# Norm sums of 256 columns in two matmuls, norms begun by chunks' first terms, and attention's last branch in two halves

## The reference

```python
def rms_norm(x, w):                       # rmsnorm of the second block is the same
    return x * lax.rsqrt(jnp.mean(x * x, axis=-1, keepdims=True) + 1e-6) * w

def hybrid_mixer(h, w_in, dn_conv, ...):  # layers 0 and 1
    proj = h @ w_in
    (dn_qkv, dn_z, dn_b, dn_a, ret_q, ret_k, ret_v, ret_g, pool_u, gates) = split(proj)
    qkv = silu(causal_depthwise_conv(dn_qkv, dn_conv))      # 1536 features
    beta = sigmoid(dn_b)
    g = -exp(dn_A_log) * softplus(dn_a + dn_dt_bias)
    ...                                   # delta rule, retention, pooling: o_dn, o_ret, o_pool
    y = gt[0] * (o_dn @ w_branch_dn) + gt[1] * (o_pool @ w_branch_pool) + gt[2] * (o_ret @ w_branch_ret)
    return y @ w_out

def first_block(x, ...):
    for l in range(2):
        m = hybrid_mixer(rms_norm(x, mix_pre_norm[l]), ...)
        x = x + rms_norm(m, mix_post_norm[l])
        h = rms_norm(x, ffn_pre_norm[l])
        x = x + rms_norm((silu(h @ w_gate) * (h @ w_up)) @ w_down, ffn_post_norm[l])
    return x

def hybrid_mixer_2(u, pos, w_in, ..., w_a, w_b, w_c, w_o):   # layers 2 and 3
    ...                                   # three attentions: o_a, o_b, o_c
    g = sigmoid(gates)                    # 3 x 1024 features
    merged = g[0] * (o_a @ w_a) + g[1] * (o_b @ w_b) + g[2] * (o_c @ w_c)
    return merged @ w_o

def second_block(h, ...):
    for l in range(2):
        h = h + hybrid_mixer_2(rmsnorm(h, attn_norm[l]), ...)
        u = rmsnorm(h, mlp_norm[l])
        h = h + square(relu(u @ w_up[l])) @ w_down[l]
    return rmsnorm(h, final_norm)
```

## Time and profile before

| what | value |
|---|---|
| time, median of 3 runs | 1926.45 us (1924.01 to 1933.04) |
| the profiled execution: its time | 1926.13 us |
| its span in the trace | 1924.3 us |
| PE busy | 1887.5 us, 98% |
| ACT, DVE, POOL busy | 50%, 64%, 15% |
| waits of PE for other engines, all | about 30 us |

### The profile page before, as it was taken

How to read it: one execution, slowest core, us unless ns; L and a number is a source line. 1 busy time by engine, 2 the same in 40 slices (tenths; PEclk the granted TensorE clock), 3 DMA queues, 4 the chain that set the end, 5 groups by cost and what they waited for, 6 DMA issues and landing times.

```text
span 1924.3 us, 35105 instructions
## 1 busy us (share of the span) xinstructions
PE 1887.5 (98%) x14820; PEld 1800.8 (94%) x14820; DVE 1237.3 (64%) x1669; ACT 961.8 (50%) x1383; POOL 295.6 (15%) x168
## 2 busy tenths in 40 slices
PE   7999999999999999999999999999999999999998
PEld 7999998998899999999988999999999999999998
DVE  6874566665589545767647675577646684567643
ACT  5533455444563345554445445655534444656633
POOL 0050221000003103200001352310000353220000
PEclk9999999999999999999999999999999999999999
DMA  6443344656455323655665553446655663345663
GB/s 232 158 145 104 120 152 136 214 194 208 134 162 165 110 99 121 208 174 180 194 199 177 176 183 121 132 154 202 192 186 172 215 194 120 131 158 182 194 196 104
DMA packets 92156, 317.50 MB, mean 165 GB/s; under 512 B 11744, under 2 KB 12896, under 8 KB 91744
## 3 DMA queue, kind: packets, MB, share of 16 engines
q1 hardware_dynamic: 91424, 314.69, 50.1%
q10 hardware_dynamic: 576, 0.57, 0.1%
HBM read 304.99 MB, written 1.05 MB: 159 GB/s over the span
## 4 chain that ended last, share of the span: by engine, by line
PE 84%; DVE 11%; ACT 3%; issue 1%; DMA 0%; SPq 0%; DVEq 0%; ACTq 0%
PE bank L1901 82%; DVE wlo L1076 5%; DVE area L1076 3%; ACT area L618 1%; DVE area L1082 1%; ACT whi L624 1%; PE bank L2367 1%; PE bank L2099 1%; DMA raw<-in_weights 0%; DVE area L1562 0%; DVE area L1079 0%; DVE area L1560 0%; PE bank L2385 0%; ACT hh L618 0%; DVE hl L1082 0%
## 5 line engine op out<-in xcount | busy, mean ns | idle before, releaser
L1076 DVE TENSOR_TENSOR wlo<-raw,whi 128x1024 fp32r<-128x1024 f32 x518 | 659.0, 1286 | 422.1 <-ACT whi L624 421.5
L1901 PE MATMUL bank<-hh,whi 128*128 128x256 f32 x2928 | 834.6, 285 | 20.6 <-DVE wlo L1076 12.9
L1901 PE MATMUL bank<-hl,whi 128*128 128x256 f32 x2928 | 817.6, 279 | 0.0
L1901 PE MATMUL bank<-hh,wlo 128*128 128x256 f32 x2928 | 817.5, 279 | 0.0
L624 ACT CAST whi<-raw 128x1024 fp32r<-128x1024 f32 x572 | 589.0, 1046 | 403.2 <-PE bank L1901 378.0
L1901 PEld LDWEIGHTS bank<-hh,whi 128*128 128x128 f32 x2928 | 556.2, 190 | 36.2 <-DVE wlo L1076 16.8
L1901 PEld LDWEIGHTS bank<-hl,whi 128*128 128x128 f32 x2928 | 554.9, 190 | 2.0 <-issue 1.9
L1901 PEld LDWEIGHTS bank<-hh,wlo 128*128 128x128 f32 x2928 | 554.7, 189 | 0.0
L1691 POOL TENSOR_TENSOR area<-area 128x512 f32<-128x512 f32 (+4 forms) x90 | 136.9, 1530 | 1010.2 <-ACT area L618 678.8
L1901 PE MATMUL bank<-area 128*128 128x128 f32 (+5 forms) x1544 | 200.2, 289 | 1.0 <-DVE area L1130 0.7
L1691 POOL TENSOR_TENSOR wlo<-raw,whi 128x1024 fp32r<-128x1024 f32 x54 | 134.2, 2487 | 429.8 <-ACT whi L624 429.8
(11 more groups left out here) (124 smaller groups left out, 1887.4 us busy)
## 6 DMA issues: line engine op xcount, KB each, us to landing
raw<-in_weights SPq DMA_DIRECT2D x572, 512.0 KB, 4.0
area<-area SPq DMA_DIRECT2D x96, 64.0 KB, 3.8
area<-area SPq DMA_DIRECT2D x16, 128.0 KB, 3.9
cst<-in_const SPq DMA_DIRECT2D x1, 1188.0 KB, 6.1
cst<-in_const SPq DMA_DIRECT2D x1, 1024.5 KB, 5.7
xT<-in_x SPq DMA_DIRECT2D x4, 256.0 KB, 8.0
out<-xT SPq DMA_DIRECT2D x4, 256.0 KB, 2.9
area<-in_lev SPq DMA_DIRECT2D x2, 384.0 KB, 5.7
```

The source lines that it names most:

```text
L1076: return v.tensor_tensor(dst, x, y, op)
L1901: return e.matmul(ps, x, y, start=start, stop=stop, skip_group_check=skip)
```

## The change

It has four parts.

1. *Norm sums.* The squares are added down to 256 columns before PE sees them (three additions of 1024, 512 and 256 columns on DVE for the norms in `SUMMED`, else four on POOL), and `norm_sum` is two matmuls of 128 columns. It stands after the fourth chunk instead of the second; the first two evacuations wait for it. In qkv the SW matmuls and the start of the delta rule stand two chunks later as well.
2. *Transitions* (norms in `TURNED`). PE takes the first two chunks together, part by part, first only the terms with hh (`parts`), then the terms with hl. DVE makes all eight additions and then lows 1 to 3; POOL makes low 0. ACT splits one chunk before the highs and one between highs and squares (`AROUND`).
3. *Last branch.* B2H and B2L are made in two halves, from turns 8 and 9 apart, in buffers of their own; PE's first wc chunk takes the first half for both its tiles, then the second (`last_branch`). wb's last evacuations come before the splits of their step.
4. *Gates.* sigmoid(x) is (tanh(x/2) + 1)/2: ACT makes tanh, DVE multiplies the bank by gate + 1, and the factor 1/2 goes into FH and FL. Tanh and Exp are taken from one table set in attention.

```diff
 # ACT
+                if fn is AF.Tanh:
+                    tables(EXPTANH)
+                elif fn is AF.Ln or fn is AF.Exp and table[0] != EXPTANH:
                     ln_exp()
...
-                    if hook and len(chunks) == 2:
+                    if hook and step < 2:
+                        waiting, done = waiting + done, []
+                    if hook and step == 2:
                         hook()
+                        done = waiting + done
...
+                split(around[0])
                 for j in range(4):
                     high(then, j, *v_norm.at("added", then, j))
+                split(around[1])
                 for j in range(4):
+                    if j == 3:
+                        a.wait_ge(*g_norm.at("low", then))
                     square(then, j)
...
+            def gate(name, L, j):
+                projection, dst = BRANCH[name][2:]
+                a.wait_ge(*v_evac.at(projection, L, 2 * j + 2))
+                d = dst[:, 512 * j:512 * j + 1024]
+                act(d, d, AF.Tanh, scale=0.5).then_inc(*a_br.up("gate", name, L, j))
...
+                def wc_high(j):
+                    a.wait_ge(*a_att.at("OO", L, 8 + j))
+                    a.copy(BR2[0][:, 2 * j:2 * j + 2, :], v3(BRANCH["wc"][1])[:, 2 * j:2 * j + 2, :]).then_inc(*a_br.up("high", "wc", L, j))
 # DVE
+            def squares(norm):
+                v.wait_ge(*a_norm.at("square", norm, 3))
+                for n in (4 * T, 2 * T, T):
+                    x = tt(SQ2[:, 0:n], SQ2[:, 0:n], SQ2[:, n:2 * n], OP.add)
...
+                for j in range(4):
+                    add(j)
+                for j in range(1, 4):
+                    low(then, j)
...
-                    tt(gate[:, c], b[:, :], gate[:, c], OP.mult).then_inc(*v_evac.up(name, L, m0))
+                    stt(gate[:, c], gate[:, c], 1.0, b[:, :], OP.add, OP.mult).then_inc(*v_evac.up(name, L, m0))
 # POOL
+            def low(norm):
+                g.wait_ge(*a_norm.at("high", norm, 0))
+                for k in (0, 1):
+                    x = g.tensor_scalar(SQ2[:, (6 + k) * T:(7 + k) * T], xT[:, k, :], GAIN[norm][:, k:k + 1], None, OP.mult)
+                x.then_inc(*g_norm.up())
+                g.wait_ge(*g_norm.now())
+                tt(hl[:, 0:2, :], v3(pair(SQ2, 3)), hh[:, 0:2, :].bitcast(F32), OP.subtract).then_inc(*g_norm.up("low", norm))
 # PE
+            def parts(job, ready, norm):
...
+                for k in range(8):
+                    e.wait_ge(*(a_norm.at("high", norm, k // 2) if k else a_norm.at("first", norm)))
+                    for m in range(2):
+                        i = (at + m) % RING
+                        mm(bank[b][:, m * T:(m + 1) * T], whi[:, i, 128 * k:128 * k + 128], hh[:, k, :], (m, k) == (0, 0), False, True)
+                        mm(bank[b][:, m * T:(m + 1) * T], wlo[:, i, 128 * k:128 * k + 128], hh[:, k, :], False, False, True)
+                for j in range(4):
+                    e.wait_ge(*ready(j))
+                    for m in range(2):
+                        for k in (2 * j, 2 * j + 1):
+                            x = mm(bank[b][:, m * T:(m + 1) * T], whi[:, (at + m) % RING, 128 * k:128 * k + 128], hl[:, k, :], False, k == 7, True)
...
-                for j in (1, 3):
-                    e.wait_ge(*g_norm.at("squares", norm, j))
-                    for k in range(2):
-                        x = mm(bank[b][:, 0:T], C("ones"), pair(SQ2, j)[:, k * T:(k + 1) * T], (j, k) == (1, 0), (j, k) == (3, 1))
+                e.wait_ge(*(v_norm if norm in SUMMED else g_norm).at("squares", norm))
+                for c in (0, 128):
+                    x = mm(bank[b][:, c:c + 128], C("ones"), SQ2[:, c:c + 128], True, True)
```

More of the change, by code:

```diff
@@ L26 @@
 EXPLN = "natural_log_exp_and_others"
+EXPTANH = "exp_and_others"
 CONST1 = {}
@@ L255 @@
              "last": 7}
+TURNED = ("ffnpre0", "mixpre1", "ffnpre1", "attn2")
+SUMMED = ("mixpre0",) + TURNED
+AROUND = {j.first + c for j in JOBS.values() if isinstance(j, Job) and (j.name, j.layer) in (("gu", 0), ("qkv", 1), ("gu", 1), ("q2a", 2)) for c in (2, 3)}
 BY_TOKEN = ("mixpre0", "mixpre1", "attn2", "attn3")
@@ L857, in first @@
                 qkv = project("qkv", L, conv, hook)
+                next(qkv)
+                next(qkv)
                 next(qkv)
@@ L1093, in project @@
                             split(s)
-                    if hook and len(chunks) == 2:
+                    if norm and step == 0:
+                        squares(norm)
+                    if hook and step < 2:
+                        waiting, done = waiting + done, []
+                    if hook and step == 2:
                         hook()
+                        done = waiting + done
                     for m0 in done:
@@ L1318, in evac @@
                         merge(L, m0 // 2 - 1)
+                if between:
+                    for step, (chunks, done) in enumerate(JOBS[name, L].steps()):
+                        for i in chunks:
+                            for s in STAGED[i]:
+                                if step == 0:
+                                    split(s)
+                        for m0 in done:
+                            evac(m0)
+                            if m0 == 4:
+                                between()
+                        for i in chunks:
+                            for s in STAGED[i]:
+                                if step:
+                                    split(s)
+                        yield
+                    return
                 yield from project(name, L, evac)
@@ L1877, in second @@
                     all_squares("attn3")
-            for j in range(4):
-                squares("mixpre0", j)
             g.wait_ge(s_head, 16)
@@ L1973, in project @@
                                 x.then_inc(*proj.up(*full))
+                    if hook and step == 2:
+                        hook()
                     if after:
@@ L2282, in sums @@
                     norm_sum(norm)
-                qkv = project("qkv", L, *h, sums)
+                qkv = project("qkv", L, *h, sums, norm=norm if L else None)
+                next(qkv)
+                next(qkv)
                 next(qkv)
```

160 lines of the change are left out of this document (104 added, 56 removed).

## The result

| | before | after |
|---|---|---|
| time, median of 12 runs each | 1927.03 us (1923.18 to 1935.53) | 1918.13 us (1907.28 to 1925.58) |
| ratio of the runs | | 0.9937, 95% interval 0.9915 to 0.9959 |
| the profiled execution: time, span | 1926.13, 1924.3 us | 1915.12, 1913.3 us |

The kernel is faster by 0.4 to 0.9%, 8 to 16 us. Measured again later (run 10), the same two kernels gave 0.9974 (0.9953 to 0.9995). The two profiled executions are 11.0 us apart. The prediction said 1910 and a range from 1901 to 1920.

A forecast was written before the change was run, and what follows sets the result against it. The prediction took PE, working 98% of the span, to bound the kernel. Its terms summed to -18.3 us against 1926.13, so 1907.8; 2 us for PE's pace made it 1910 us, range 1901 to 1920.

The forecast's parts named there:

- the first rival: A long product falls into PE's slow pace; two of them falling gives 1917 to 1921; chance 0.14.
- Transitions, four times -3.2, with the sum: At each transition PE's first pair ends 1.6 us earlier and the norm sum saves 1.6, together 3.2 us.
- Low 0 on POOL: At the transitions, 2.6 us cover POOL's two multiplications, up to 1.3 each, before PE wants low 0; 0.4 taken.
- qkv: Layers 0 and 1: two extra table loads, 2.56 us a layer; net +1.3, and -0.7 with layer 1's transition.
- wc, -2.2 each: Layers 2 and 3: PE's waits at wb's last bank and wc go, 2.67 us, less 0.5 for DVE's queue.
- up, -1.8 each; attn3, -1.25: Layers 2 and 3: norm sum saves 1.25 and PE's fourth-chunk wait goes, 1.8 each; attn3's sum saves 1.25.
- The additions on DVE: Norm sums: DVE's three additions take 2.1 to 4.1 us, hidden since PE reaches the sum 5.4 us later.
- Pace, +2 us: PE's pace, 117.2 or 112.8 ns a matmul, changes at restarts after waits; 2 us added, spread some 5 either side.
- That qkv doesn't lose: Rival: in qkv the loads fit into ACT's idle 2.14 us a period; -5.1, giving 1905; chance 0.10.
- the loss at wc: Rival: at wc PE waits for DVE's wlo as long as for B2L; loses 4.4, giving 1914; chance 0.06.
- That a table load holds up ACT for longer than its row: Rival: in qkv ACT's pipeline empties before each load; four cost 5.1 us more, giving 1915; chance 0.03.
- PE's pace as a reason for "slower": Rival: work in fast products falls into the slow pace too, 4.4 ns a matmul; 1936 and more; chance 0.03.

The follow-up runs named there:

- run 10: The changed kernel, no edit, timed again beside the kernel before: 1919.39 us, ratio 0.9974.
- Run 3: The changed kernel with each silu of qkv one bank later on ACT, so one table load per layer instead of three: 1904.85 us.
- Run 7: The changed kernel with wb's splits ahead of its evacuations on DVE and B2L's second half right after the attention's last turn: 1924.53 us.
- run 6: The changed kernel, but PE takes wc's first chunk tile row by tile row with the whole input, as before: 1926.62 us.
- Run 11: The changed kernel with the old norm sums (POOL adds squares, four matmuls of 256 columns) at the new place behind the fourth chunk: 1936.28 us.
- Run 8: The changed kernel with Sigmoid in place of the hyperbolic tangent in the gates: 1930.57 us.
- run 4: The changed kernel with qkv's new norm sum, first evacuations, small weights and delta rule start back behind the first two chunks: 1922.09 us.
- run 12: The changed kernel with its first part undone wholly, old norm sums behind the first two chunks: 1931.15 us, ratio 1.0021.
- run 5: The changed kernel with low 0 made by DVE instead of POOL at the transitions: 1906.38 us.
- run 9: The changed kernel with the edits of Run 3 and run 5 together: 1915.91 us, ratio 0.9960.

## Why the prediction was right, and where it was off

**The direction and the range.** Faster was given 0.81 and came; 1918.13 lies in the range and outside the forecast's own 1904 to 1915 (its sum with +5 of pace is 1913). It is where the first rival stood, "a long product falls into the slow pace", 1917 to 1921, which had 0.14 and was booked as "same". That the time is still in the range owes something to luck: of the 16 us forecast, 8.9 came in the first measurement and 5.4 in the second.

**The sum, term by term.** It said -18.3; the traces of the changed kernel say -15.6, -13.2 and -17.7.

- *Transitions, four times -3.2, with the sum.* Measured -2.5 to -3.0 each in all three traces. The steps were right: PE went straight on, then ran against the highs. The wait at k=2 was worked out at 0.45 us, and it is 0.32; at k=4 and k=6, where its times left 0.05 us and nothing, PE didn't wait. What was missing is 0.36 of wait for the third chunk's wlo, since POOL's subtraction held up one of DVE's lows for 1.04 us. The text had this contention, at "a few tenths, within their slack".
- *Low 0 on POOL.* I took 0.4 us for a multiplication with 0.3 to 1.3 as bounds; it is 0.91. The cover held.
- *qkv.* This is the term of the edits that was furthest off. It said 2.56 us of loads per layer, layer 0 +1.3, mixpre1 and qkv 1 together -0.7. Measured: layer 0 +0.9 to +5.5; transition and qkv of layer 1 together +1.2 to +3.9. Without the half clock that is about +1.7 to +2.3 and +0.9 to +1.9, so layer 0 missed by under 1 us and layer 1 by some 2. The lockstep was right, and so were three loads. From the third bank's evacuation (539.18 before, 541.07 after, in DVE's timeline) to the sixth's (558.98 and 564.81) the chain takes 3.94 us more, not 2.56: the three small exponentials now stand in it as well (0.7 us), and some 0.7 more lie between the records. The other miss is the start: I let the chain begin 3.2 us earlier, and against the transition ahead of it, it began 2.46 earlier. Run 3 gives the price of the whole, 3 us per layer. And the longer wait, 2.09 us, has a price of its own, below.
- *wc, -2.2 each.* Measured -3.1 and -4.7. The 0.5 that I took back for DVE's queue never came; both wlo were in time. In layer 3, 1.6 more are the clock: before, PE fell to half clock after its wait there. Run 7 shows that the order on DVE did it, which the prediction named, and run 6 that PE's two steps did little.
- *up, -1.8 each; attn3, -1.25.* Measured -1.7, -1.3 to -1.7, and -0.7 to -1.2 at attn3's start. Run 11 has 1.26 to 1.29 for a norm sum where nothing waits.
- *The tangent for itself: nothing.* Against the kernel before that holds, as far as the traces show: it has no wait at wa. Run 8's 1.6 us are what the tangent saves the changed kernel, whose gate comes later.

**The additions on DVE, "hidden".** They are (2.4 us, PE at its fourth chunk), but only since the sum stands so late; run 4 shows the 3.9 us of wait when it doesn't.

**Pace, +2 us.** This is the second term that was mis-sized. In the 11 traces of kernels with the new place of the sum the pace part against the profile of before is -2.9 to +15.6, mean +8.4; for the changed kernel alone +4.7, +7.8 and +9.1, mean 7.2. Before has 0 and +3.6. So by these five traces the changed kernel runs some 5 us slower by pace, and 15.5 - 5.4 = 10 us are left, against the medians' 8.9 in the first measurement and 5.4 in the second. The second leaves some 4.7 us that the traces don't account for. I had written that nothing pushes all restarts one way. At one place something does: in layer 1's gu the pace went with the place of the norm sum in all 14 traces, which is 1.6 us. The largest part of the 5 is up and down of layer 3, fast in both traces of before and slow in the changed kernel's three, 6 us; run 12 was slow there too, with the sum at its old place, and runs 3 and 5 were fast, so what sets it is open. With two traces of before it can be chance. In layer 2's wo a part ran at 118 ns in the changed kernel's three executions and none in before, but none in runs 3, 4, 5 and 9 either. Long waits were followed by either pace.

**The other rivals.** That qkv doesn't lose is out, and so is the loss at wc. That a table load holds up ACT for longer than its row is out too: the load at 543.07 has 1.28 us in its row and the silu starts at 544.36, 1.29 after it. The Trainium skill, page "ScalarE: Activation LUTs", section "What ACT_TABLE_LOAD costs", adds some 1380 ns of drain to each switch; in this trace there is no room for it. PE's pace as a reason for "slower" was a real mechanism, but in none of the traces was there enough of it: the most is run 6's 15.6 us, of the 18.5 that would have eaten the gain.

## What to carry to other kernels

Where two engines run in lockstep and PE follows them, count every instruction that a moved hook brings into that loop, not only the dear one: three exponentials and two table loads cost 3 us a layer in place of 2.6, and taking them out gave two thirds of it back (the rest went into a wait of the delta rule). A matmul begun earlier pays only if all that is due next is early too: the turned transitions gain 2.8 us with the norm sum two chunks later, and in run 12, with the old sum at its old place, they lose 1.6 to 3.1. And before work goes from one engine to another, look at which instructions of the two run at the same time: here the mean of a row hid that one low in six was held up and the others not at all. Before a gain of half a per cent is booked, take several traces and part steady intervals from the rest, since one program's executions lie 10 to 20 us apart by pace alone.

## What the runs showed of the hardware

**Two paces of PE at full clock.** Steady matmuls of 256 columns start 113.3 or 117.8 ns apart, nothing between, with a granted clock of 1.00 for both; those of 512 columns in down 228.9 or 233.3. A stretch keeps its pace to the next wait or foreign matmul. The same program drew either in some stretches (gu of layer 0: 113 and 118 in two executions of before), and some stretches had one pace in every execution (layer 1's gu). Up and down of one layer cost 5.7 to 6.0 us more at the slow one.

**A wait of about 2 us can halve the clock, and by chance.** PE's windows in the changed kernel behind its wait of 2.09 us:

```profile
557.70:559.00 1.30, 1.30 (x6) 1.30 (x7) 1.30 (x2) 0.00 (x0) 0.00 (x0) 0.53 0.37 72
559.00:561.10 2.10, 2.10 (x12) 2.10 (x11) 2.03 (x5) 1.60 (x4) 0.00 (x0) 0.50 0.76 267
561.10:564.00 2.90, 2.90 (x26) 2.90 (x26) 2.52 (x5) 2.35 (x3) 0.00 (x0) 0.98 0.36 136
```

The clock is at 1.2 GHz, 0.50, for some 15 matmuls at 213 ns from PE's restart on, which costs 1.6 us on top of the wait. In all traces here, 12 of 22 such waits (1.9 to 2.4 us idle) in the middle of a product were followed by this and 10 were not, the same place now one way and now the other. The eight waits of 1.57 us at the transitions of before never were; of the four of 2.7 us in run 12, ahead of a norm sum, three were. In layer 3 of before the wait at wc was, in both its traces, so that what was worth 3.1 us in layer 2 was worth 4.7 there. The clock also fell at places without such a wait, in every trace.

**POOL and DVE hold each other up.** DVE's lows of 256 columns, with two inputs xT and hh, have records of 0.48 us. The one that starts 0.1 us after POOL's subtraction of 512 columns (1.34 us) has 1.52 and ends 0.28 us after it, in all 40 transitions of the ten traces that have it; in runs 5 and 9, without POOL there, no low of a transition has more than 0.48. The other way round, POOL's addition of 512 columns took 1.30 us in before and 3.76 in run 12, where DVE's lows and splits ran beside it. DVE's additions to xT beside POOL's multiplications kept their 0.39 us from start to start. The Trainium skill, page "GPSIMD Engine Reference", section "Specifications", has POOL share its SBUF interfaces with DVE, with contention for DVE instructions with two SBUF inputs; these rows agree. A POOL multiplication of 256 columns with one input took 0.91 us. Here all this cost more than POOL's help gave.
